# A more compact last level of the triangular inverse, and four changes of order around it, in a one-core kernel of two transformer blocks

## What is computed

```python
kb = k * beta[..., None]
A = jnp.where(strict, jnp.einsum('bhntk,bhnsk->bhnts', kb, k) * Lmat, 0.0)
T = lax.linalg.triangular_solve(eye + A, jnp.broadcast_to(eye, A.shape),
                                left_side=True, lower=True, unit_diagonal=True)
u = jnp.matmul(T, v * beta[..., None])
w = jnp.matmul(T, kb * jnp.exp(gam)[..., None])
...
v_new = u_c - jnp.einsum('bhtk,bhkv->bhtv', w_c, S)
```

## Time and profile before

| | |
|---|---|
| time, median of 3 executions | 1425.29 us (1425.22 to 1426.19) |
| the profiled execution's own time | 1425.13 us |
| its span, first to last instruction | 1423.4 us |
| TensorE (PE) busy | 98% of the span, 9926 matmuls |
| VectorE (DVE) busy | 72% |
| ScalarE (ACT) busy | 56% |
| granted TensorE clock | 0.999 of full speed |
| pipeline stages 1 to 7 | 7 passes of the loop, 52.7 us each |

### The profile page before, as it was taken

One profiled execution on the slowest core, in us unless ns is written; L12 is line 12 of the kernel. 1 busy time (PEld: TensorE's weight loads), 2 busy tenths in 40 slices (PEclk: granted clock), 3 DMA queues, 4 the chain that ended last, 5 costly groups with the idle time before them and its releaser, 6 DMA issues.

```text
span 1423.4 us, 26906 instructions
## 1 busy us (share of the span) xinstructions
PE 1398.3 (98%) x9926; PEld 1294.7 (91%) x9926; DVE 1021.2 (72%) x1525; ACT 801.4 (56%) x1289; POOL 28.5 (2%) x73
## 2 busy tenths in 40 slices
PE   8999999999999999999999999999999999999998
PEld 8999999988999878888899999999999899788887
DVE  5786777676545586666788888888888855676665
ACT  4345454644444454444568788788788743544443
POOL 6000000000000000000000000000000000000000
PEclk9999999999999999999999999999999999999999
DMA  8565454555555646566574444534533356566661
GB/s 257 146 179 144 132 137 152 185 197 176 180 191 192 208 118 207 177 186 197 147 179 119 123 114 118 135 102 117 146 98 111 92 157 212 155 181 186 198 205 61
DMA packets 304638, 224.90 MB, mean 158 GB/s; under 512 B 10418, under 2 KB 288068, under 8 KB 304580
## 3 DMA queue, kind: packets, MB, share of 16 engines
q1 hardware_dynamic: 304580, 224.09, 53.7%
HBM read 223.02 MB, written 1.05 MB: 157 GB/s over the span
## 4 chain that ended last, share of the span: by engine, by line
PE 85%; DVE 8%; ACT 2%; DVEq 2%; issue 1%; POOL 0%; ACTq 0%; POOLq 0%
PE G L1778 12%; PE G L1780 12%; PE G L1779 12%; PE M L1802 5%; PE M L1783 5%; PE M L1784 5%; PE M L1785 5%; PE G L1802 5%; PE M L1804 3%; PE G L1804 3%; DVE w_lo L1053 3%; DVEq L1050 2%; PE M L1778 2%; PE M L1780 2%; PE M L1779 2%
## 5 line engine op out<-in xcount | busy, mean ns | idle before, releaser
L1053 DVE TENSOR_TENSOR w_lo<-w_raw,w_hi 128x2048 fp32r<-128x2048 f32 (+1 forms) x208 | 475.1, 2287 | 195.5 <-ACT w_hi L576 190.6
L576 ACT ACTIVATE w_hi<-w_raw 128x2048 fp32r<-128x2048 f32 x207 | 394.7, 1909 | 202.6 <-PE G L1780 134.3
L1778 PE MATMUL G<-xa,w_hi 128*128 128x256 f32 x1480 | 439.2, 297 | 1.8 <-DVE w_lo L1053 1.4
L1780 PE MATMUL G<-xa,w_lo 128*128 128x256 f32 x1480 | 418.4, 283 | 0.0
L1779 PE MATMUL G<-xa,w_hi 128*128 128x256 f32 x1480 | 418.1, 282 | 0.0
L1778 PEld LDWEIGHTS G<-xa,w_hi 128*128 128x128 f32 x1480 | 282.1, 191 | 6.8 <-issue 5.2
L1779 PEld LDWEIGHTS G<-xa,w_hi 128*128 128x128 f32 x1480 | 282.3, 191 | 2.1 <-issue 1.7
L1780 PEld LDWEIGHTS G<-xa,w_lo 128*128 128x128 f32 x1480 | 281.6, 190 | 0.1
L1783 PE MATMUL M<-w_hi,xb_hi 128*128 128x512 f32 x304 | 118.9, 391 | 0.9 <-DVE xb_lo L1053 0.9
L1784 PE MATMUL M<-w_lo,xb_hi 128*128 128x512 f32 x304 | 118.7, 390 | 0.0
L1785 PE MATMUL M<-w_hi,xb_lo 128*128 128x512 f32 x304 | 118.3, 389 | 0.0
(11 more groups left out here) (373 smaller groups left out, 2382.7 us busy)
## 6 DMA issues: line engine op xcount, KB each, us to landing
w_raw<-in_w_in SPq DMA_DIRECT2D x166, 512.0 KB, 4.7
w_raw<-in_ffn_w_in SPq DMA_DIRECT2D x88, 512.0 KB, 5.0
w_raw<-in_w_ff SPq DMA_DIRECT2D x64, 512.0 KB, 4.3
w_raw<-in_ffn_w_out SPq DMA_DIRECT2D x44, 512.0 KB, 4.7
w_raw<-in_w_out SPq DMA_DIRECT2D x16, 512.0 KB, 4.1
w_raw<-in_w_branch_gdn SPq DMA_DIRECT2D x16, 512.0 KB, 5.1
w_raw<-in_w_branch SPq DMA_DIRECT2D x12, 512.0 KB, 4.2
w_raw<-in_w_branch_hgrn SPq DMA_DIRECT2D x8, 512.0 KB, 4.1
```

The costliest lines, as they stand in the source:

```text
L576: nc.scalar.activation(w_hi[:, slot, :], w_raw[:, slot, :], ACT.Copy).then_inc(hi_ready, 1)
L1053: return v.tensor_tensor(dst, src, hi.bitcast(F32), ALU.subtract)
L1778: mm(out_, w[0], x[0], start=first, stop=False)
L1780: return mm(out_, w[1], x[0], start=False, stop=last_)
```

## The change

1. Level 6 works on packed operands. `inv_z(6)` is two products of 128 columns (both heads at once, from a new packed copy `n21`), `inv_t(5)` two transposes in place of four, `inv_w(6)` two products of 64 columns. VectorE's masked merge (L1561) becomes two plain copies. What the full-bank copy did for the diagonal quarters is done by a new function, `y_diagonal`, with four ScalarE copies; `compact(5)` and the copy into `n21` are new on ScalarE too.
2. On ScalarE, `split_j(1)`, the conversion of a weight chunk, moves from between `level_exp(7)` and `level_exp(8)` to behind `y_copy(5)`.
3. On TensorE, `delta_turned(i)` moves behind `quarter(19)`, the transposes at L2409 move behind `quarter(22)`, and `values_turned` moves from the end of a stage to the first level of the next.
4. In stage 8 one conversion on ScalarE moves to the start, its `w_low` on VectorE is cut into two halves (`w_low_half`).
5. Behind the stages, `delta_turned(GH)` and `delta_out(GH)` come one tile and one pair of tiles later.

```diff
@@ ScalarE
-                if l == LEVELS - 1:
-                    nc.scalar.activation(halved(zi.rearrange("p i e c -> p (i e c)"), l, 0), packed(M[:, 3, 0:T], l),
-                                         ACT.Copy).then_inc(zc_ready, 1)
-                    return
@@ y_copy
-                    nc.scalar.activation(yi.rearrange("p i e c -> p (i e c)"), M[:, 5, :], ACT.Copy).then_inc(yy_ready, 1)
+                    nc.scalar.activation(yc[:, :, HD:P], M[:, 5, 0:T].rearrange("p (i c) -> p i c", i=TT)[:, :, HD:P],
+                                         ACT.Copy).then_inc(yy_ready, 1)
+
+            def y_diagonal():
+                if not main:
+                    return
+                for side in range(2):
+                    half = slice(HD * side, HD * side + HD)
+                    for e in range(2):
+                        ins = nc.scalar.activation(yi[half, :, e, half], M[HD * e:HD * e + HD, 5, 0:T].rearrange(
+                            "p (i c) -> p i c", i=TT)[:, :, half], ACT.Copy)
+                ins.then_inc(yy_ready, 1)
@@ head on ScalarE
             if main:
                 level_exp(7)
-            if gemm:
-                split_j(1)
-            else:
-                act_split(c0 + 5 + RING - 6)
-            if main:
                 level_exp(8)
+            compact(5)
             z_copy(6)
             y_copy(5)
+            split_j(1)
+            y_diagonal()
...
+                nc.scalar.activation(n21, nt[:, :, :, HD:P], ACT.Copy)
@@ VectorE
                     dve.wait_ge(wt_done, i)
-                    dve.sem_inc(waited, 1)
-                    v.copy_predicated(halved4(yi, l, 1), halved(lmask[:, l, :].bitcast(I32), l, 1).unsqueeze(1).to_broadcast(shape),
-                                      packed(M[:, 5, 0:T], l).rearrange("p (x n) s -> p x n s", x=4)).then_inc(yy_ready, 1)
+                    for e in range(2):
+                        ins = v.tensor_copy(yi[0:HD, :, e, HD:P],
+                                            M[HD * e:HD * e + HD, 4, 0:P].rearrange("p (i c) -> p i c", i=TT))
+                    ins.then_inc(yy_ready, 1)
...
-            if n == 1:
+            if n == 2:
                 delta_out(GH)
@@ TensorE
                 if l == LEVELS - 1:
-                    four(3, nt, xi, l, 0, zz_done)
+                    for b in range(TT):
+                        ins = mm(M[:, 3, P * b:P * b + P].rearrange("p (e c) -> p e c", e=2), n21[:, b, :, :].rearrange("p e c -> p (e c)"),
+                                 xi[:, b, :, 0:HD], start=True, stop=True)
+                    ins.then_inc(zz_done, 1)
...
                 if l == LEVELS - 1:
-                    four(5, zi, yi, l, 1, wt_done)
+                    for b in range(TT):
+                        ins = mm(M[:, 4, HD * b:HD * b + HD], zd[:, b, :, :].rearrange("p e c -> p (e c)"), yc[:, b, HD:P],
+                                 start=True, stop=True)
+                    ins.then_inc(wt_done, 1)
...
             quarter(18)
+            quarter(19)
             if main and gemm:
                 delta_turned(i)
-            quarter(19)
...
-            if tile == 3:
+            if tile == 4:
                 delta_turned(GH)
```

More of the change, by code:

```diff
@@ L224, in emit @@
     ntc = grid(vn1.rearrange("p e c -> p (e c)"), i=TT, e=2, c=HD)
-    xc = grid(yi.rearrange("p i e c -> p (i e c)")[:, 2 * P:4 * P], i=TT, e=2, c=HD)
+    xc, n21 = (grid(mix(2 * P), i=TT, e=2, c=HD) for _ in range(2))
     assert mix.at <= ARENA - 320 and late_end <= ARENA - 320, (mix.at, late_end)
@@ L908, in head @@
                 nc.scalar.activation(sgz, G[:, 0, :].rearrange("p (e t) -> p e t", e=2), ACT.Copy).then_inc(evac[0], 1)
-            if main and gemm:
+            if main:
                 act_split(c0 + 5 + RING - 6)
@@ L1060, in w_low, with w_low_half @@
             low_of(w_lo[:, slot, :], w_raw[:, slot, :], w_hi[:, slot, :]).then_inc(lo_ready, 1)
+        def w_low_half(c, h):
+            dve.wait_ge(hi_ready, c + 1)
+            part = slice(CHUNK // 2 * h, CHUNK // 2 * (h + 1))
+            ins = low_of(w_lo[:, c % RING, part], w_raw[:, c % RING, part], w_hi[:, c % RING, part])
+            if h == 1:
+                ins.then_inc(lo_ready, 1)
         def x_low_half(n, h):
@@ L1462, in _ @@
                             beta.rearrange("p i (h e) -> p i h e", e=2), sign, None, ALU.mult)
-        v.memset(zi, 0.0)
         v.memset(zd, 0.0)
@@ L1602, in head @@
                 o_low(2, 4, GH - 1)
+                w_low_half(FIRST["yh"] + 2, 0)
             tap(1, 0)
@@ L1616, in head @@
             decayed(7)
+            decayed(8)
             if not gemm:
-                w_low(c0 + 5 + RING - 6, i, 6)
-            decayed(8)
+                w_low_half(FIRST["yh"] + 2, 1)
             tap(1, 2)
@@ L2250, in level, with values_turned @@
                 ins.then_inc(lev_done, 1)
-            def four(out_bank, lhs, rhs, l, side, done):
+            def values_turned():
+                if not main:
+                    return
+                pe.wait_ge(evac[1], EV_HEADS[1] + 3 + (i - 1) * 3)
                 for b in range(TT):
[L2254 to L2258, removed]
+                    ins = nc.tensor.transpose(M[:, 1, P * b:P * b + P], hvt[:, P * b:P * b + P], ident[:])
+                ins.then_inc(hvt_done, 1)
             def inv_z(l):
@@ L2280, in inv_w @@
                 pe.wait_ge(zc_ready, l + (i - 1) * 6)
-                pe.wait_ge(yy_ready, l + (i - 1) * 7)
+                pe.wait_ge(yy_ready, l + (i - 1) * 8)
                 if l == LEVELS - 1:
-                    four(5, zi, yi, l, 1, wt_done)
+                    for b in range(TT):
+                        ins = mm(M[:, 4, HD * b:HD * b + HD], zd[:, b, :, :].rearrange("p e c -> p (e c)"), yc[:, b, HD:P],
+                                 start=True, stop=True)
+                    ins.then_inc(wt_done, 1)
                     return
@@ L2292, in inv_t @@
                     return
[L2293 to L2299, removed]
+                pe.wait_ge(xc_ready, l + 1 + (i - 1) * 6)
                 for b in range(TT):
-                    for e in range(2):
-                        at = T * b + P * e
-                        ins = nc.tensor.transpose(M[:, 5, at:at + P], xi[:, b, e, :], ident[:])
+                    ins = nc.tensor.transpose(M[:, 5, P * b:P * b + P], xc[:, b, :, :].rearrange("p e c -> p (e c)"), ident[:])
                 ins.then_inc(yt_done, 1)
@@ L2315, in head @@
                     level(at_quarter[2 * l - 2])
+                if l == 1:
+                    values_turned()
                 inv_w(l)
@@ L2325, in head @@
             if main:
-                pe.wait_ge(yy_ready, i * 7)
+                pe.wait_ge(yy_ready, i * 8)
                 for e in range(2):
@@ L2403, in head @@
             quarter(21)
+            quarter(22)
             if gemm:
@@ L2410, in head @@
                 ins.then_inc(t_done, 1)
-            quarter(22)
             quarter(23)
[L2413 to L2417, removed]
         head(0, True, False)
```

## The result

The changed kernel takes 1437.17 us (median of 6 executions, 1435.51 to 1438.05), the kernel before 1425.24 us (6 executions, 1424.94 to 1426.19). The ratio is 1.0082, 95% interval 1.0069 to 1.0095: slower by 0.8%, 11.9 us. The forecast was 1434, with a range of 1424 to 1438. The profiled execution is the fastest of the six, 1435.51 us, 10.4 us above the profiled one of before; its span is 1433.8 us.

A forecast was written before the change was run, and what follows sets the result against it. TensorE is full, but a chain through VectorE closes each pass. From 1425.13 us, +10.5 for seven passes, -0.1 in stage 8 and -1.65 behind the stages gave 1433.9, rounded to 1434; range 1424 to 1438.

The forecast's parts named there:

- What closes a pass: Loop pass: a chain through VectorE closes it; TensorE, though full, waits 0.18 us at inv_z(2) for VectorE's level 1 merge.
- Part 1, TensorE: Level 6 on TensorE: fewer matmul records save 0.47 us on Z, 0.49 on W, 0.17 on transposes, 1.1 per head.
- Part 2, ScalarE: ScalarE around level 6: added copies and the moved conversion make the Silu table load 2.0 us late, 1.7 of it added work.
- What is late next: After ScalarE: eh at 937.6, VectorE's r1 1.2 us late, TensorE stands 1.5 us for it and goes on 0.4 late.
- Part 3: Moved transposes: VectorE waits for delta_turned until 950.4, 1.7 us late; about 0.2 is absorbed at L1703.
- +1.5 us for each of 7 passes: Loop total: all three engines shift by the same amount each pass, +10.5 us.
- Parts 4 and 5: Stage 8 and behind the stages: gains of 0.1 us in stage 8 and 1.65 from delta_turned(GH)'s removed wait.
- A: Whole kernel as forecast: 1.1 to 1.9 us more per pass, 1431 to 1437 us; chance 0.70.
- D: Rival, worse: lateness also starves projections of a converted chunk, 0.5 us or more per pass, 1437.5 or more; chance 0.07.
- C: Rival, faster: ScalarE's lateness does not reach the pass's end; 1419.9 us, or 1415.7 if VectorE closes nothing; chance 0.15.
- B: Rival: ScalarE hardly late, leaving the wait for moved delta_turned, about 0.6 us per pass, 1427.6 us; chance 0.08.

The follow-up runs named there:

- e3_both_back: Changed kernel with split_j(1) and delta_turned(i) back at their old places, packed level 6 and tail kept: 1422.55 us, ratio 0.9983.
- e7_full_transpose: e3_both_back with level 6's packed operands taken from a full transposition, no compact(5), one copy in place of y_diagonal's four: 1422.60 us, ratio 0.9978.
- e5_delta_only: Kernel before with only delta_turned(i) moved behind quarter 19 in the loop: 1434.32 us, ratio 1.0062.
- e1_split_back: Changed kernel with only the conversion split_j(1) back between level_exp(7) and level_exp(8) on ScalarE: 1429.42 us, ratio 1.0026.
- e6_no_diagonal: Changed kernel without y_diagonal, leaving out the copying of the diagonal quarters of the inverse: 1428.27 us, ratio 1.0022.
- e4_tail_only: Kernel before with only the change behind the stages, delta_turned(GH) and delta_out(GH) later: 1423.53 us, ratio 0.9990.
- e9_full_transpose_early: e7_full_transpose with the transposes of L2409 again ahead of quarter 22: 1421.05 us, ratio 0.9973.
- e10_early_warm: e9_full_transpose_early with two more idle products in stage 8, ahead of inv_w(1) and inv_z(2): 1420.92 us, ratio 0.9969.

## Why the prediction was right, point by point

**What closes a pass.** That TensorE, busy in 98%, was not what closes the pass was the step that decided the sign. It holds: e3_both_back has TensorE's saving and a pass of 52.5, e7_full_transpose has most of it with ScalarE in time and 52.41, and e5_delta_only has none of the added work and a pass of 53.8.

**Part 1, TensorE.** `inv_z(6)` now begins at 931.91 and `inv_t(5)` at 933.07 in the shown pass, 1.16 us apart where it was 1.62: 0.46 less, 0.47 forecast.

```profile
931.91 0.61 PE L2285 MATMUL M<-arena 128*128 128x128 f32 x4
932.27 0.36 PE L1792 MATMUL G<-xa,w_hi 128*128 128x256 f32 x1
...
933.07 0.38 PE L2315 MATMUL M<-ident,arena 128*128 128x128 f32 x2
933.21 0.36 PE L1792 MATMUL G<-xa,w_hi 128*128 128x256 f32 x1
...
934.22 0.56 PE L2301 MATMUL M<-arena 128*128 128x64 f32 x4
934.59 0.36 PE L1792 MATMUL G<-xa,w_hi 128*128 128x256 f32 x1
```

From start to start Z now takes 0.36 us (0.82 before), the transposes 0.14 (0.35) and W 0.37 (0.84): 1.14 us less, 1.1 forecast. Four records of 128 columns (Z) and four of 64 (W) cost the same, so the saving is by matmuls, not by columns. By the table of the Trainium skill, page "TensorE: Matmul & The Clock Gate", section "Back-to-back issue gap", nothing would have been saved on Z; the trace contradicts that table where it is used alone. The same section says that in a stream of weight loads and matmuls both set the spacing, and that fits. The busy line does not show the saving: it falls by 0.35 us a pass only (52.52 to 52.17), at least in part because ahead of a wait the whole length of a matmul counts, not only what the next one leaves of it.

**Part 2, ScalarE.** The table load is 1.96 us late (forecast 1.95 to 2.0), `y_diagonal` takes 1.11 (forecast 1.1; the formula of the Trainium skill, page "ScalarE: Activation LUTs", section "What ACT_TABLE_LOAD costs", gave 0.9). The share of the conversion's place is the 7.8 us of e1_split_back, that of `y_diagonal` the 8.9 of e6_no_diagonal. Together they are more than the whole 11.9, so they overlap; no run undoes both.

**What is late next.** VectorE's wait at the new L1656 is 2.01 us, and `r1` is 1.3 late, 1.2 forecast. TensorE's wait for it was put at 1.5 and is 1.02, since it already stands 0.27 us ahead of the cross term, a wait that the sum left out, and because VectorE's `vn0` comes only 0.39 us sooner (26.40 us after the merge of level 1, 26.79 before), TensorE's products 1.1. The wait at `inv_z(2)` is 0.92, about 1.2 forecast.

**Part 3.** The wait ahead of `delta_out` is 0.65 us, about 0.5 forecast. The step that was mis-sized is the sum "+1.5 us for each of 7 passes": it is 1.79. The pieces: `delta_out` 2.0 late instead of 1.7 and 0.2 absorbed as forecast, which leaves 1.8. Each link was a little short: `eh` is 2.1 late against 1.95, `r1` 1.3 against 1.2, and `delta_turned` begins 41.2 us after the merge of level 1, where the forecast's 949.7 makes it 40.9. In the sum that is 1.9 us (12.4 against 10.5) of the 3.3 between 1433.9 and 1437.2.

**Parts 4 and 5.** The tail gave 1.5 us in e4_tail_only (1.65 forecast). In the profiles the seven passes, from the merge of level 1 in stage 1 to that in stage 8, take 380.88 us against 368.44, 12.44 more. From the latter to the end it is 302.6 us against 304.4, 1.75 less, as forecast for both parts together; less the tail's 1.5, stage 8 gained 0.2 (0.1 forecast). The 0.3 us that are missing to the measured 10.4 lie ahead of the first of these merges (750.30 against 750.59), which differs as much between profiles of the other runs. TensorE waits 0.63 us there for the ScalarE result of the earlier trace rows:

```profile
1154.62 0.44 PE L2355 MATMUL M<-ident,arena 128*128 128x128 f32 x2 [0.63 <-ACT arena L908]
...
1162.26 0.60 PE L2188 MATMUL M<-ident,arena 128*128 128x128 f32 x4
```

The forecast's times imply a wait of about 1.0 (1142.55 - (1142.67 - 1.1)). In the last row `delta_turned(GH)` has none.

**What was not in it.** The median lies 1.66 us above the profiled execution. The prediction took both to be the same, as they are in the kernel before. The likely cause is the clock in stage 8, where the change lengthened TensorE's waits at `inv_w(1)` from 0.48 to 0.93 us and at `inv_z(2)` from 1.36 to 2.03; e1_split_back and e6_no_diagonal fell behind the same two waits, the profiled execution of the changed kernel did not. The median lies 0.2 us above A's own range (1431 to 1437) and 0.3 under the price of D, so the number alone does not tell A from D; the traces do.

**The rivals.** C (faster) fell as it was set up: ScalarE had 0.4 us of slack, not 1.9. With the slack restored (e7_full_transpose), VectorE does close the pass and little is gained: 0.28 us a pass, not the 0.5 of C, and 0.15 in e3_both_back, where VectorE still waits for `eh`. B needed ScalarE hardly late: e1_split_back is near that case (VectorE waits 0.62 us for `eh`) and has a pass 0.68 above the old one, 0.6 forecast for it. No wait for a converted chunk appeared in the loop, so D did not come.

## What to carry to other kernels

An engine that is busy in 98% of the span may still be the one that waits: look for the wait, however short, that returns in every pass, and follow what ends it. Work moved from a full engine to one with idle time is free only where that idle time lies ahead of something nobody waits for; here ScalarE had 10 us of idle time per pass and 0.4 us of slack at the one place that counted. A filler such as a weight conversion belongs into a wait of its engine, and the copies that others wait for must then not come behind it.

## What the runs showed of the hardware

- For fp32 matmuls with a new weight load each, 64 moving columns cost as much as 128 (four records in 0.37 and 0.36 us in the changed kernel), and the saving comes from fewer matmuls.
- TensorE's clock fell to 1.2 GHz behind two waits of 0.94 and 0.92 us with 1.1 us of work between them (e7_full_transpose), for some 3 us, and stayed up in the profiled execution of the kernel before with 0.48 and 1.36. With 0.93 and 2.03 it fell in e1_split_back and e6_no_diagonal and stayed up in the changed kernel, so the length of the waits alone does not decide it. The spread of the executions was 1.8 us in e9_full_transpose_early (seven) and 0.4 in e10_early_warm (six), which has two short idle products more ahead of and between these waits; that they are the reason is not shown.
